# Streaming encoder step on one core: input loads in smaller pieces, channel sums on VectorE, layer norm scaled behind the inverse

## The reference, cut to what matters

```python
h = rms_norm(x, norm_mix_g)                  # over 1024 channels
proj = h @ w_in                              # qkv, z, beta, decay, glu
qkv = silu(causal_dwconv(qkv, width 4)); q, k, v = split; q, k l2-normalised
o, s_new = gated_delta_chunked(q, k, v, g, beta, s0)   # unit triangular solve, then chunks in turn
o = rms_norm(o, w_onorm) * silu(z)
c = causal_dwconv(glu part, width 31) + b_dw
c = silu(layer_norm(c, ln_g, ln_b))          # over 512 channels
x = x + concat(o, c) @ w_out
x = x + moe_top4_of_32(rms_norm(x))          # gate/up, clamped SwiGLU, down, per expert
y = rms_norm(x)
```

## Time and profile before

| | |
|---|---|
| median of three runs | 1280.99 us |
| profiled execution: time, span | 1280.59 us, 1278.8 us |
| mean granted TensorE clock | 0.981 of full |
| PE busy | 1180.8 us, 92% of the span |
| DVE busy | 449.5 us, 35% |
| ACT busy | 242.4 us, 19% |
| POOL busy | 77.8 us, 6% |
| HBM read | 428.5 MB, mean 339 GB/s over the span |

### The profile page before, as it was taken

One profiled execution on the slowest core, in us unless ns is written; L12 is line 12 of the kernel. 1 busy time (PEld: TensorE's weight loads), 2 busy tenths in 40 slices (PEclk: granted clock), 3 DMA queues, 4 the chain that ended last, 5 costly groups with the idle time before them and its releaser, 6 DMA issues. The chain is left out here.

```text
span 1278.8 us, 16454 instructions
## 1 busy us (share of the span) xinstructions
PE 1180.8 (92%) x6532; PEld 561.2 (44%) x6548; DVE 449.5 (35%) x886; ACT 242.4 (19%) x426; POOL 77.8 (6%) x81
## 2 busy tenths in 40 slices
PE   6999999998999999999998989899999998998986
PEld 3666688757443433333332324434343333333332
DVE  2989633215553233231322222332223323131224
ACT  2135545132211101011110101011010101111012
POOL 1100143263000000000000000000000000000000
PEclk9989999897899999999999999999999999999998
DMA  9422210036999999999999999799999999999994
GB/s 378 152 84 81 89 26 2 9 148 226 374 406 426 427 431 428 427 428 430 428 427 429 429 427 425 332 375 427 429 428 427 428 429 428 427 429 428 427 428 182
DMA packets 34792, 433.74 MB, mean 339 GB/s; under 512 B 4704, under 2 KB 5088, under 8 KB 8928
## 3 DMA queue, kind: packets, MB, share of 16 engines
q1 hardware_dynamic: 32336, 428.64, 79.8%
q0 software_dynamic: 800, 3.08, 0.7%
q10 hardware_dynamic: 1616, 1.45, 0.4%
HBM read 428.50 MB, written 4.65 MB: 339 GB/s over the span
## 5 line engine op out<-in xcount | busy, mean ns | idle before, releaser
L1867 PE MATMUL bank<-ring,win 128*64 128x512 f32 x1984 | 442.3, 595 | 48.9 <-DMA ring<-in_w_gate_up 47.9
L1867 PEld LDWEIGHTS bank<-ring,win 128*64 128x64 f32 x1984 | 138.1, 137 | 335.5 <-issue 231.4
L1890 PE MATMUL bank<-ring,win 128*64 128x512 f32 x992 | 222.1, 600 | 0.3 <-issue 0.3
L1327 DVE TENSOR_SCALAR win<-bank 128x512 f32<-128x512 f32 x33 | 22.8, 691 | 403.1 <-PE bank L1867 381.2
L1890 PEld LDWEIGHTS bank<-ring,win 128*64 128x64 f32 x992 | 70.2, 138 | 133.9 <-issue 127.8
L828 ACT ACTIVATE win<-win 128x512 f32<-128x512 f32 x33 | 20.8, 630 | 448.3 <-DVE win L1327 448.3
L836 ACT ACTIVATE win<-bank 64x512 f32<-64x512 f32 x64 | 37.9, 592 | 279.0 <-PE bank L1890 264.9
L1261 DVE TENSOR_TENSOR win<-win,qkvc 128x1024 f32<-128x1024 f32 x16 | 19.6, 1226 | 143.0 <-ACT qkvc L854 143.0
L1321 DVE TENSOR_TENSOR xt<-xt,bank 128x512 f32<-128x512 f32 x108 | 67.8, 680 | 2.1 <-PE bank L1840 2.1
L1846 PE MATMUL bank<-qkvc,win 128*128 128x512 bf16 x272 | 64.1, 379 | 4.4 <-issue 2.5
L963 DVE SCALAR_TENSOR_TENSOR cb<-ring,par,cb 128x384 f32<-128x384 f32 x120 | 66.7, 612 | 0.8
(11 more groups left out here) (305 smaller groups left out, 1073.2 us busy)
## 6 DMA issues: line engine op xcount, KB each, us to landing
ring<-in_w_gate_up SPq DMA_DIRECT2D x127, 2048.0 KB, 24.4
ring<-in_w_down SPq DMA_DIRECT2D x63, 2048.0 KB, 21.9
win<-in_w_in SPq DMA_DIRECT2D x3, 2048.0 KB, 7.4
ring<-in_w_in SPq DMA_DIRECT2D x2, 2048.0 KB, 13.5
win<-in_w_out SPq DMA_DIRECT2D x2, 2048.0 KB, 8.6
win<-in_w_in SPq DMA_DIRECT2D x4, 512.0 KB, 10.1
ring<-in_w_gate_up SPq DMA_DIRECT2D x2, 1024.0 KB, 10.0
out_ss<-ring POOLq DMA_DIRECT2D x1, 2048.0 KB, 10.7
```

The source lines that it names most:

```text
L1327: dve.tensor_scalar(g_s, bank[low], LIMIT, None, ALU.min).then_inc(g, 1)
L1867: mm = pe.matmul(bank[half][a * BLK:(a + 1) * BLK], xs[:, k], ring[:, c:c + 512], start=False, stop=(k == KD - 1), skip_group_check=True)
L1890: mm = pe.matmul(bank[7][a * BLK:(a + 1) * BLK], actT[:, q * P + j * BLK:][:, 0:BLK], ring[:, c:c + 512], start=(k == 0), stop=(k == KD - ...
```

## The change

- SP loads x in three pieces (tiles 0 and 1, 2 and 3, 4 to 7), with job 0's weights in two halves between them; each has its own semaphore. Jobs 1 to 3 follow as before.
- The eight squared tiles are added on DVE (seven dependent additions behind the gain multiplies), and PE does one product with ones instead of eight.
- Both channel sums of the layer norm likewise: three additions on DVE into spare parts of `oT`, then one product instead of four. The first stands ahead of tile 2's decays, the second at the end of step 3.
- The reciprocal and scaling of the layer norm move on DVE from the end of step 5 to behind the last step and behind the two multiplications of `s_qg`. ACT's four SiLUs move behind the copies of the first new values and of the rows for tiles 1 and 2, ahead of the first `out_root`.

```diff
+        ln_sums = [oT[:, i * T:(i + 1) * T] for i in range(2)]
+        X_PIECES = (0, 2, 4, KD)
+        def x_piece(k):
+            return sum(k >= x for x in X_PIECES[1:])
 # SP
-            half = KD * T // 2
-            sp.dma_start(hT[:, 0:half], xT[:, 0:half]).then_inc(s_xT, 16)
-            sp.dma_start(hT[:, half:], xT[:, half:]).then_inc(s_xT2, 16)
-            for j in range(4):
-                sp.dma_start(wjob[0][:, j], w_in[:, j * KD * P:(j + 1) * KD * P].rearrange("p (k n) -> p k n", k=KD))\
-                  .then_inc(s_job0[j], 16)
+            def load_x(i):
+                a, b = X_PIECES[i], X_PIECES[i + 1]
+                sp.dma_start(hT[:, a * T:b * T], xT[:, a * T:b * T]).then_inc(s_xT[i], 16)
+            def load_job(j, k0, k1, done):
+                sp.dma_start(wjob[0][:, j, k0:k1], w_in[:, (j * KD + k0) * P:(j * KD + k1) * P]
+                             .rearrange("p (k n) -> p k n", k=k1 - k0)).then_inc(done, 16)
+            load_x(0)
+            load_job(0, 0, KD // 2, s_job0[0])
+            load_x(1)
+            load_job(0, KD // 2, KD, s_job0[4])
+            load_x(2)
+            for j in range(1, 4):
+                load_job(j, 0, KD, s_job0[j])
 # ACT
-            for c in range(CC):
-                act.wait_ge(s_lnd, c + 1)
-                act.activation(cb3[:, c], cb3[:, c], ACT.Silu, bias=col("ln_b", c), scale=col("ln_g", c))\
-                   .then_inc(s_conf, 1)
...
             for n in (1, 2):
                 act.wait_ge(s_wt, n)
                 act.activation(flat(x_, n), bank[4 * (n - 1)], ACT.Copy, scale=-1.0).then_inc(s_wte, 1)
+            for c in range(CC):
+                act.wait_ge(s_lnd, c + 1)
+                act.activation(cb3[:, c], cb3[:, c], ACT.Silu, bias=col("ln_b", c), scale=col("ln_g", c))\
+                   .then_inc(s_conf, 1)
             out_root(0)
 # DVE, behind the eight gain multiplies
+            for k in range(1, KD):
+                dve.wait_ge(s_sq, k + 1)
+                ins = dve.tensor_tensor(sq3[:, 0], sq3[:, 0], sq3[:, k], ALU.add)
+                if k < KD - 1:
+                    link(ins)
+            ins.then_inc(s_added, 1)
             dve.wait_ge(s_rt, 1)
...
+            def add_channels(i, x):
+                link(dve.tensor_tensor(ln_sums[i], x[:, 0], x[:, 1], ALU.add))
+                link(dve.tensor_tensor(ln_sums[i], ln_sums[i], x[:, 2], ALU.add))
+                dve.tensor_tensor(ln_sums[i], ln_sums[i], x[:, 3], ALU.add).then_inc(s_lnp, 1)
...
                     conv_qkv(10)
+                if n == 2:
+                    add_channels(0, cb3)
                 b0 = GRAM_BANK[n]
...
-                if step == NT + 2:
-                    dve.wait_ge(s_lroot, 1)
+                if step == NT:
                     dve.wait_ge(s_lsq, CC)
-                    link(dve.reciprocal(lroot, lroot))
-                    for c in range(CC):
-                        dve.tensor_tensor(cb3[:, c], cb3[:, c], lroot, ALU.mult).then_inc(s_lnd, 1)
+                    add_channels(1, lsq3)
             for n in (1, 2):
                 dve.wait_ge(s_de, N_DONE)
                 dve.tensor_tensor(tile4(d_, n), qkv3[:, 0:H, n * P:(n + 1) * P], tile4(eg_, n), ALU.mult).then_inc(s_qg, 1)
+            dve.wait_ge(s_lroot, 1)
+            link(dve.reciprocal(lroot, lroot))
+            for c in range(CC):
+                dve.tensor_tensor(cb3[:, c], cb3[:, c], lroot, ALU.mult).then_inc(s_lnd, 1)
 # PE
-                for k in range(KD):
-                    pe.wait_ge(s_sq, k + 1)
-                    mm = pe.matmul(bank[4][:, 0:T], mat("ones"), sq3[:, k], start=(k == 0), stop=(k == KD - 1))
-                mm.then_inc(s_ssum, 1)
+                pe.wait_ge(s_added, 1)
+                pe.matmul(bank[4][:, 0:T], mat("ones"), sq3[:, 0], start=True, stop=True).then_inc(s_ssum, 1)
...
                 for k in range(KD):
+                    if j == 0 and k == KD // 2:
+                        pe.wait_ge(s_job0[4], 16)
...
-                    for c in range(CC):
-                        mm = pe.matmul(bank[6][:, 0:T], mat("ones"), lsq3[:, c], start=(c == 0), stop=(c == CC - 1))
-                    mm.then_inc(s_ln2, 1)
+                    pe.wait_ge(s_lnp, 2)
+                    pe.matmul(bank[6][:, 0:T], mat("ones"), ln_sums[1], start=True, stop=True).then_inc(s_ln2, 1)
...
-                    pe.wait_ge(s_dwc, CC)
+                    pe.wait_ge(s_lnp, 1)
                     pe.wait_ge(s_a1d, NT)
-                    for c in range(CC):
-                        mm = pe.matmul(bank[6][:, 0:T], mat("ones"), cb3[:, c], start=(c == 0), stop=(c == CC - 1))
-                    mm.then_inc(s_ln, 1)
+                    pe.matmul(bank[6][:, 0:T], mat("ones"), ln_sums[0], start=True, stop=True).then_inc(s_ln, 1)
```

More of the change, by code:

```diff
@@ L281, in stream_step @@
         rr = epst[:, 8:8 + NT]
-        s_xT, s_cst, s_par, s_hist, s_state = (sem(x) for x in ("xT_in", "consts_in", "params_in", "hist_in", "state_in"))
+        s_xT = [sem(f"xT_in{i}") for i in range(3)]
+        s_cst, s_par, s_hist, s_state = (sem(x) for x in ("consts_in", "params_in", "hist_in", "state_in"))
         s_win = [sem(f"win_in{i}") for i in range(3)]
-        s_job0 = [sem(f"first_win_in{i}") for i in range(4)]
-        s_xT2, s_evd, s_uh, s_kqt = sem("xT_in_upper"), sem("first_taken"), sem("u_pasts"), sem("qk_turned")
+        s_job0 = [sem(f"first_win_in{i}") for i in range(5)]
+        s_evd, s_uh, s_kqt = sem("first_taken"), sem("u_pasts"), sem("qk_turned")
         s_xt, s_gff, s_wr = sem("x_in"), sem("gffn_in"), sem("router_in")
@@ L291, in stream_step @@
         s_eps = sem("eps_set")
+        s_added = sem("squares_added")
+        s_lnp = sem("ln_channels_added")
         s_sq, s_ssum, s_rt, s_h = sem("x_squared"), sem("x_sum"), sem("x_root"), sem("hT_ready")
@@ L587, in _ @@
             for k in range(KD):
-                act.wait_ge(s_xT if k < KD // 2 else s_xT2, 16)
+                act.wait_ge(s_xT[x_piece(k)], 16)
                 act.activation(sq3[:, k], hT3[:, k], ACT.Square).then_inc(s_sq, 1)
@@ L933, in _ @@
             for k in range(KD):
-                dve.wait_ge(s_xT if k < KD // 2 else s_xT2, 16)
+                dve.wait_ge(s_xT[x_piece(k)], 16)
                 dve.tensor_scalar(gx3[:, k], hT3[:, k], col("g_mix", k), None, ALU.mult).then_inc(s_h, 1)
+            for k in range(1, KD):
[4 more added lines that the diff above has]
+            ins.then_inc(s_added, 1)
             dve.wait_ge(s_rt, 1)
```

## The result

The changed kernel takes **1271.16 us** (median of 6 runs, 1267.88 to 1275.01) against 1281.01 (6 runs, 1280.58 to 1283.55) for the kernel before: ratio 0.9921, interval 0.9907 to 0.9934, 9.9 us faster. Forecast were 1268.6, with 1264.8 to 1274.8 as range. Two things are to be explained: 2.6 us of gain that did not come, and runs that spread over 7 us where those of before spread over 3. The profiled execution took 1272.87, with a span of 1271.0.

The account below looks back on a forecast made before the run. The expert weight stream paces the end, released by PE's progress before 355 us. Savings of 6.8 + 1.97 + 1.93 + 1.7 = 12.4 us gave a median of 1268.6, range 1264.8 to 1274.8.

Parts of the forecast that it names:

- The mechanism: PE's progress before 355 us releases the expert weight stream; a saving counts if it makes that stream run earlier.
- Loads: Front: last x piece at 10.4 us, PE starting at about 6.4, job 0 ending at about 14.2 instead of 18.4.
- The rival of slow pieces: Front loads: gaps between small transfers halve the rate, last piece 6.0 us later, median 1274.6; chance 0.06.
- Channel sums: Front: seven adds on VectorE take 4.2 us; job 1 begins at 16.8 instead of 23.64, 6.8 us earlier.
- The bounds of 5.7 to 7.6: Range in us for job 1's 6.8 us gain, from the bounds of landing and adds.
- The predicted wait behind job 0: PE waits for VectorE's adds from 14.2 to 16.1 us, with job 1 queued behind.
- Layer norm sums: Inverse stage: two sums cut to two passes each, saving 1.97 and 1.93 us; their adds cost nothing.
- Scaling: End of the inverse: scaling moved off the last subtractions lets PE go on 1.7 us earlier, at least 1.3.
- The cover: Own states on PE hide the later normed rows of the first output: 5.8 us of cover, 2.3 left.
- the fifth: Granted clock, from the own states to 320 us: 3 to 4 us either way, time of fall not computable.
- The second rival: PE stays at slow pace into job 1: another 5.3 us at half pace costs 2.6, 1271.2; chance 0.12.
- the working on the own states: Of 64 own-state passes, 36 ran fast at 0.11 us and 28 at twice that, for 9.84 us.

Follow-up runs that it names:

- run 6: Changed kernel with the adds of tiles 1 to 3 moved ahead of the gain multiplies of tiles 4 to 7: 1269.98 us, ratio 0.9905.
- run 5: Kernel before with only the layer norm's reciprocal and scaling moved behind the last subtractions and the SiLUs moved later: 1277.54 us, ratio 0.9979.
- runs 1 and 7: 1: changed kernel again, unedited, 1271.69 us. 7: changed kernel plus two unused 512-column products ahead of the last six combining products, 1269.76 us.
- runs 3, 6 and 9: 3: kernel before with only squares added on VectorE, 1277.47 us; 9: changed kernel, eight first-output-tile products between own states, 1268.14; 6: see run 6.
- both with filling: Unused 512-column products: two ahead of the last combining products in the changed kernel, 1269.76 us; three edits together, plus three before routing masks, 1263.13.

## Why the prediction was right, and where its sizes were off

The mechanism held: all the change's steps are on PE's way to the weight stream, and what was gained there arrives at the end of the stream. In the changed kernel 10.57 us at the first expert are still 10.65 at the last weights, a thousand us later, and the first expert weights behind the heads' wait are issued at 265.06 instead of 275.29, 10.2 us earlier where 12 were forecast. Point by point, against the profile:

- *Loads.* The last x piece landed at 10.98 (10.4 taken), PE started at 6.45 (6.4), job 0 ended at 14.4 (14.2). The rival of slow pieces is out: the first 10 us moved at nearly the same rate in either kernel, 304 and 301 GB/s:

```profile
0.00:10.00 10.00, 3.55 (x6) 2.01 (x7) 1.52 (x5) 3.16 (x5) 2.08 (x15) 1.00 0.82 301
```

By the rule that stood behind that rival, of the Trainium skill, "DMA: Bandwidth & Descriptors", section Bandwidth, the last piece would have come about 10 us later (an estimate by its 138 GB/s for 64 KB: 21 us for 2.89 MB); these rows disagree with that. That section of the Trainium skill gives 138 GB/s for 64 KB and 341 for 1 MB and nothing between; the pieces here are of 256 to 768 KB with several in flight, so what is refuted is the use of the small figure for them.

- *Channel sums.* Adds 4.12 (4.2), the product at 16.53 (16.1), job 1 at 17.28 (16.8). The front gave 6.36, not 6.8: the x piece came 0.58 late, and 0.14 was won behind it. The bounds of 5.7 to 7.6 were added wrongly: 0.2 and 0.4 on the one side and 0.8 and 0.9 on the other give 6.2 to 8.5, which holds the measured figure as well. The predicted wait behind job 0 is there, 2.13 us; run 6 shows what it is made of.
- *Layer norm sums.* The first ran 171.30 to 172.00, 0.70 with the release of what follows, and the second 0.65: 1.93 and 1.93 gained (1.97 and 1.93). That PE goes from instruction to instruction in the inverse stage was read too broadly: it also waits 2.12 us for ACT ahead of the first inverse step, before and after, and the change does not touch that wait.
- *Scaling.* 1.67 (1.7), and run 5 alone shows 1.65. The cover held: DVE made the normed rows from 219.5 to 220.7, and PE was ready for them at 224.0.
- *Sum of work:* 6.36 + 1.93 + 1.93 + 1.67 = **11.9** of 12.4.
- *The grant* took back the rest: 11.9 - 1.65 (gate columns: 10.2 us at half speed instead of 6.8) - 2.56 (combining products) = 7.7, and the span is 7.8 shorter. At the own states 0.88 was lost and behind them 0.86 won back, since the same 10.2 us of half speed began 1 us earlier against the work.

So the term that was mis-sized is the fifth: put at zero in the sum, it measured 4.2 us lost in the profiled run (in the median some 2, from 11.9 of work and 9.9 measured). "3 to 4 us either way" was the right size, and its sign was put at zero; but I placed it between the own states and 320 us, and it came at two other places: at and behind the gate columns, whose stretch of 6.8 us in before I had not looked at, and in the last 8 us, where nothing hides a loss. The second rival occurs as well, as one outcome among the runs of one kernel (runs 1 and 7), for 1.7 us. A single row of a profile gave one outcome of something that varies from run to run: with the front of before, the gate columns' stretch was 6.8 us in two profiles and 10.2 in a third. Nor did the working on the own states close: 36 passes at 0.11 and 28 at 0.22 are 10.1 us, where 9.84 were read. The range held the result because it left room for 4 us of clock against the forecast; that this room was used at other places than those it was worked out for is luck.

What stays open: why the combining products fell to half speed in the profiles of after (twice), and of runs 3, 6 and 9, and not in those of before and of the others. The same instructions precede them, and the same wait of 0.88 us. The times of the fall fall into groups: counted from the start of the combining products, 2.3 to 2.7 us in those five; 6.2 to 6.7 us, that is behind their end, in the six others without filling; 8.6 us in both with filling. So what differs is when the grant changes against the same work. Whether the filling moved it, and what sets the moment, no run here tells.

## What to carry to other kernels

Work out a saving along the engine's way to the point from which a transfer stream paces the rest, and read there whether it arrived; the end of the run mixes it with the clock. Where two savings meet at one product, each alone may be worth its full price and both together less, since one uncovers the other's dependent chain: start such a chain on what has landed, before the last piece. Where products of few columns stand in a row, try them between wide ones: two such changes of order and the earlier adds, with not an instruction more, took the gain from 10 to 20 us.

## What the runs showed of the hardware

- TensorE's grant fell to 0.50 (1.2 GHz) while or after it ran long rows of narrow products: at the gate columns (48 passes of 8 columns) in all ten profiles that have them in a row, for 3.4 to 10.2 us, and at the own states (64 passes of 32 columns) in all ten that have those in a row, for 6.8 to 10.2. With the same products between those of 384 or 512 columns it stayed at 1.00 there, in three of three profiles for either place; PE was busy throughout in either order. The Trainium skill, "TensorE: Matmul & The Clock Gate", Part 1, says the hardware sets the clock by how busy the array has been; the profile's busy share, full in both orders, did not tell the two apart here.
- Which stretches a run gets varies between runs of one kernel (the changed kernel's mean grants of 0.982 down to 0.976 are 3.6% to 4.8% of the span at half speed), and goes with most of its spread. 3.4 us at half speed cost 1.7 where PE is the bound.
- Transfers of 256 and 384 KB in front of one of 768 moved as fast as those of 512 and 768: 301 and 304 GB/s over the first 10 us, the idle start in it.
- A dependent chain of adds of 128x384 f32 goes at 0.59 us an add (seven in 4.12), where independent ones take 0.47.
